# Output projection 1: a third unit of seven block products for the rows from 2048 on

## The chip, the cores and the metric

The kernel runs on one core of a Trainium2 chip. The metric is the device time of one execution in microseconds; the median of three runs of the kernel before is 2237.72 us (2235.79 to 2238.78).

## What is computed

A trunk of two layers on x of 512 x 2048 in float32. The first one, which the change touches, is a gated mixer with a width of 4096:

```python
def spatial_gating_layer(x, norm_g, w_in, v_norm_g, w_s, b_s, w_out):
    h = rms_norm(x, norm_g)
    u, v, z = jnp.split(h @ w_in, 3, axis=-1)      # w_in 2048 x 12288
    u = jax.nn.gelu(u)
    v = rms_norm(jax.nn.gelu(v), v_norm_g)
    ...                                            # v in chunks of 128 positions, 16 groups of 256
    mixed = jnp.einsum('gts,bcsgd->bctgd', w_causal, v) + b_s.T[None, None, :, :, None]
    y = u * mixed * jax.nn.silu(z)                 # 512 x 4096
    return y @ w_out                               # w_out 4096 x 2048: "output projection 1"
```

The second layer is forgetting attention, with an input projection of 2048 x 8208 and its own output projection of 2048 x 2048. Each layer's output is added to x.

## The kernel before

**Precision.** Each large product is made of three matmuls: high part times high part, high times low, low times high (lines 1416 to 1418 in `product`, 1593 to 1595 in `tile`). The high part is a copy in the type fp32r by ScalarE, the low part the difference, by VectorE.

**Units.** Most products run in units of 2048 rows x 1024 columns of weights. A unit does a 2 x 2 block product with seven block products instead of eight. It has 16 steps, one for each pair of row blocks k in each of two phases: 8 steps of four products (24 matmuls of 128 x 512) and 8 steps of three (18 matmuls). Units 0 to 3 (VU = 4) give v, units 4 to 11 give u and z (ZU = 8, so NU = 12), units 12 and 13 (NU, NU+1; `is_out`) the output projection for rows 0 to 2047, columns 0 to 1023 and 1024 to 2047. NS = 14. Units UB and on belong to the second layer.

**One step.** SP loads the weights into one of four raw slots (`load_step`), so it is up to four steps ahead; in the second phase also a sum from t2_rows. VectorE forms a sum in the slot (`sums`), ScalarE makes the high parts (`high`: the first tiles, then the others), VectorE the low parts (`low`: first tiles with line 1877, other tiles with line 1880). TensorE does two products behind `lo1_first` and the rest behind `lo1_ready` (`first_half`, `second_half`). In the instruction order of VectorE, `sums` of the next step stands before both low parts of this step. u_hi and u_lo have two buffers each. `sums_end`, `sum_57`, `sum_11` combine the products in buffers at the unit's end.

**What becomes of y.** y is made in eight parts of 512 columns. Unit VU+1+j gates part j: ScalarE and VectorE make y0, POOL loads v from v_rows (line 734), ScalarE scales it (`v_scale`, line 1047), TensorE mixes it (`mix`, line 1547) and turns it (`turn_y`), ScalarE takes it out of PSUM (`y_leave`) in two halves e. The last half of part j is taken out at the start of the next unit. POOL stores parts 0 to 3 to yf_rows and parts 4 to 7 to yT_rows.

**Forms.** Units 12 and 13 need sums of blocks of y ("forms"). POOL makes them in DRAM: `forms(j, n)` for n = 0 to 4 are five rounds of copies and accumulating DMAs over yf_rows (lines 704 to 714), each of which waits for the one before through the semaphore `made`, 192 a part. They are made for j = 0 to 3, in POOL's loop one part later: behind the store of part j and ahead of the loads of v. Then SP loads them (`load_form(m)`, 8 forms for x1 and 8 for x2) in units NU-1 and NU, at the steps that the tables FORM_LOAD, FORM_HIGH and FORM_LOW give, counted from the start of NU-1: 7, 8, 9, 12, ..., 29 for the load. `load_form(m)` stands behind `load_step` of that step in SP's order; SP runs in order. ScalarE and VectorE make their high and low parts (`form_high`, `form_low`).

**Products into DRAM.** part_rows holds x at first; POOL adds the units' output buffers to it by accumulating DMAs (`store_out`, 512 KB each; semaphore o_stored).

**Plain products.** Rows 2048 to 4095 (KB = 16 row blocks) are done by `tile` for each of the four column blocks f of 512: 64 tiles (B0 = 64), 12 matmuls each. The operands come from yT_rows (`load_y`, `y_high`, `y_low`), the weights through w_raw, w_hi, w_lo. `add_out(f)` adds PSUM and part_rows in acc[f]. Then acc is turned for the second layer (`turn_x`), its squares are summed, and it is stored in x2_rows.

Stretches of the profile: unit NU-1 begins at about 896 us, NU at 978, NU+1 at 1059; the plain tiles run from 1136 to 1316, then UB begins.

Of the kernel before, what the change touches and what calls it, by code (L numbers as in the profile page):

```python
# [23 lines left out]
F32 = mybir.dt.float32  # L24
# [11 lines left out]
def build_trunk(nc, x, a_norm_g, a_w_in, a_v_norm_g, a_w_s, a_b_s, a_w_out,  # L36
# [23 lines left out]
    NS = NU + D // (2 * FB)  # L60
    STEPS = NS * 2 * KP
    KB = KY - 2 * KP
    B0 = NF * KB
# [31 lines left out]
    yf_dram = nc.dram_tensor("yf_rows", [KP, P, 10, HF], F32).ap()  # L95
# [6 lines left out]
    with ExitStack() as ctx:  # L102
# [343 lines left out]
        def form_step(u, ph, k):  # L446
            return step_of(u, ph, k) - step_of(NU - 1, 0, 0)
# [35 lines left out]
        def _(sp):  # L483
# [9 lines left out]
            def weights(u, row):  # L493
                if u < VU:
                    return a_v[row:row + P, u, :, :]
                if is_out(u):
                    c = (u - NU) * 2 * FB
                    return a_out[row:row + P, c:c + 2 * FB].rearrange("r (s c) -> r s c", s=2)
# [39 lines left out]
            def load_form(m):  # L538

                n, c = FORM0 + m, m % KP  # L540
                if m == 0:
                    sp.wait_ge(made, 4 * 192)
                elif m >= 3:
                    sp.wait_ge(x1h_ready if m - 3 < KP else x2h_ready, KP + (m - 3) % KP + 1)
                sp.wait_ge(step_done, step_of(NU - 1, 0, 0) + m + 1)
                if m < KP:
                    sp.dma_start(y1_raw[:, c, :].rearrange("p (s t) -> p s t", s=4), yf_dram[c, :, 0:7:2, :])\
                        .then_inc(x_loaded[n % 3], 16)
                else:
                    sp.dma_start(z2[:, c, :, :], yf_dram[c, :, 7:10, :]).then_inc(x_loaded[n % 3], 16)  # L550

            def load_y(k):

                if k < 2:
                    sp.wait_ge(t2_stored[k], NS * KP * 8)
                    if k == 0:
                        for e in range(2):
                            sp.wait_ge(yA_stored[e], 16 * ZU)
# [5 lines left out]
            def load(i):  # L564
                f, k = i // KB, 2 * KP + i % KB
# [25 lines left out]
            for u in range(1, NS):  # L591
                for ph in range(2):
                    for k in range(KP):
                        load_step(u, ph, k)
                        if form_step(u, ph, k) in FORM_LOAD:
                            load_form(FORM_LOAD.index(form_step(u, ph, k)))
# [12 lines left out]
            for i in range(R, B0):  # L609
                f, k = i // KB, i % KB  # L610
                load(i)
                if f == 0 and k + 3 < KB:
                    load_y(k + 3)
                if f == 0 and 4 <= k < 12:
                    if k == 4:
                        sp.wait_ge(lo1_ready, STEPS)
                        sp.wait_ge(o_stored, 128)
                    t, c = k % NT, (k - 4) // NT
                    sp.dma_start(acc[c][:, t, :], part_dram[c, :, t, :]).then_inc(acc_loaded, 16)
                elif f == 1 and k < 2 * NT:  # L620
                    if k == 0:
                        sp.wait_ge(o_stored, 192)
# [1864 lines left out]
```

## Time and profile before

| | |
|---|---|
| Median of the runs | 2237.72 us |
| The profiled execution | 2240.24 us |
| Its span | 2238.5 us |
| TensorE busy | 2213.6 us, 99% |
| VectorE busy | 1716.0 us, 77% |
| ScalarE busy | 1155.0 us, 52% |
| GpSimd busy | 232.5 us, 10% |
| DMA | 520.68 MB, mean 233 GB/s |

The span is the time from the first to the last instruction of the profile. PE is TensorE, DVE VectorE, ACT ScalarE, POOL GpSimd; SPq, ACTq are queues that issue DMAs. In rows in order of time, "[4.57 <-DMA ...]" is the time that the engine stood idle before the instruction, and what ended it. Matmuls overlap, so the busy time of one is longer than its distance to the next.

### The profile page before, as it was taken

To read this page: it belongs to the slowest core of one execution; us is meant where nothing else is said; L and a number is where in the kernel's file an instruction comes from. 1 tells how busy PE (TensorE), PEld (TensorE's weight loads), DVE (VectorE), ACT (ScalarE), POOL (GpSimd) and SP (SyncE) were. 2 spreads that over 40 slices of the span, in tenths; PEclk is the share of its full clock that TensorE was granted. 3 is DMA by queue.
4 is the path that set the end of the run, shared out by engine and by line. 5 is a ranking of instruction groups with operands and counts; after the bars stand their busy time and mean duration, and the time that the engine had idled before them with its cause. 6 is when DMAs were issued, how large, how long until landed. Compare 5 with 4: busy or idle time off the path is not lost.

```text
span 2238.5 us, 27080 instructions
## 1 busy us (share of the span) xinstructions
PE 2213.6 (99%) x10197; PEld 1832.3 (82%) x10197; DVE 1716.0 (77%) x2085; ACT 1155.0 (52%) x1651; POOL 232.5 (10%) x321
## 2 busy tenths in 40 slices
PE   8999999999999999999999999999999999999999
PEld 6888888888888888888888878888788888888887
DVE  8978878877877887898753388976977878677666
ACT  6756645554554554665442455554564555443432
POOL 0011001001201200000000000110210210221110
PEclk9999999999999999999999999999999999999999
DMA  8788877778988976898985455686787798765333
GB/s 287 235 268 273 255 252 250 247 259 264 283 275 258 288 244 215 279 296 270 261 239 149 129 172 181 211 256 209 213 284 228 210 295 254 260 247 162 124 99 122
DMA packets 253793, 520.68 MB, mean 233 GB/s; under 512 B 21536, under 2 KB 37504, under 8 KB 252640
## 3 DMA queue, kind: packets, MB, share of 16 engines
q1 hardware_dynamic: 198800, 383.31, 55.8%
q0 software_dynamic: 29424, 89.47, 12.5%
q10 hardware_dynamic: 25440, 46.17, 5.4%
q8 instruction: 81, 1.33, 0.2%
q14 instruction: 48, 0.39, 0.1%
HBM read 427.58 MB, written 104.01 MB: 237 GB/s over the span
## 4 chain that ended last, share of the span: by engine, by line
PE 90%; DVE 4%; DMA 3%; ACT 1%; issue 1%; ACTq 0%; SPq 0%; POOL 0%; DVEq 0%
PE ps L1416 23%; PE ps L1418 23%; PE ps L1417 23%; PE ps L1807 2%; PE ps L1805 2%; PE ps L1806 2%; PE ps L1593 2%; PE ps L1594 2%; PE ps L1595 2%; PE ps L1721 2%; DMA raw<-in_b_w_in_dram 1%; PE ps L1667 1%; PE ps L1547 1%; DVE u_lo L1877 1%; DVE raw L1856 1%
## 5 line engine op out<-in xcount | busy, mean ns | idle before, releaser
L905 ACT ACTIVATE u_hi<-raw 128x1024 fp32r<-128x1024 f32 x352 | 372.3, 1058 | 452.8 <-PE ps L1418 355.4
L1416 PE MATMUL ps<-u_hi,x1h 128*128 128x512 f32 x1408 | 552.1, 392 | 8.8 <-DVE u_lo L1877 6.3
L1877 DVE TENSOR_TENSOR u_lo<-raw,u_hi 128x1024 fp32r<-128x1024 f32 x352 | 429.7, 1221 | 160.6 <-ACT u_hi L905 159.7
L1417 PE MATMUL ps<-u_lo,x1h 128*128 128x512 f32 x1408 | 549.5, 390 | 0.0
L1418 PE MATMUL ps<-u_hi,x1l 128*128 128x512 f32 x1408 | 549.3, 390 | 0.0
L1416 PE MATMUL ps<-u_hi,x2h 128*128 128x512 f32 x1056 | 418.0, 396 | 0.8 <-ACT e L987 0.7
L910 ACT ACTIVATE u_hi<-raw 128x512 fp32r<-128x512 f32 (+1 forms) x352 | 297.6, 845 | 230.4 <-PE ps L1418 191.7
L1418 PE MATMUL ps<-u_hi,x2l 128*128 128x512 f32 x1056 | 411.6, 390 | 0.0
L1417 PE MATMUL ps<-u_lo,x2h 128*128 128x512 f32 x1056 | 411.1, 389 | 0.0
L1880 DVE TENSOR_TENSOR u_lo<-raw,u_hi 128x512 fp32r<-128x512 f32 (+1 forms) x352 | 335.0, 952 | 41.7 <-ACT u_hi L910 40.5
L1416 PEld LDWEIGHTS ps<-u_hi,x1h 128*128 128x128 f32 x1408 | 265.2, 188 | 67.8 <-DVE u_lo L1877 9.0
L1418 PEld LDWEIGHTS ps<-u_hi,x1l 128*128 128x128 f32 x1408 | 265.3, 188 | 55.5
L1417 PEld LDWEIGHTS ps<-u_lo,x1h 128*128 128x128 f32 x1408 | 265.4, 188 | 54.2
L1856 DVE TENSOR_TENSOR raw<-raw 128x1024 f32<-128x1024 f32 x176 | 214.3, 1218 | 30.5 <-DMA raw<-in_b_w_in_dram 27.6
L1416 PEld LDWEIGHTS ps<-u_hi,x2h 128*128 128x128 f32 x1056 | 198.3, 188 | 41.8 <-issue 1.6
L1418 PEld LDWEIGHTS ps<-u_hi,x2l 128*128 128x128 f32 x1056 | 198.2, 188 | 41.8
L1417 PEld LDWEIGHTS ps<-u_lo,x2h 128*128 128x128 f32 x1056 | 198.4, 188 | 39.8
L1858 DVE TENSOR_TENSOR raw<-raw 128x512 f32<-128x512 f32 x176 | 121.6, 691 | 12.2 <-DMA raw<-t_rows 12.2
L2120 DVE TENSOR_TENSOR w_lo<-w_raw,w_hi 128x512 fp32r<-128x512 f32 x64 | 44.0, 691 | 98.3 <-ACT w_hi L1140 98.3
L2422 DVE TENSOR_TENSOR accb<-ps,accb 128x1024 f32<-128x1024 f32 x64 | 78.2, 1222 | 47.2 <-PE ps L1807 47.1
L1870 DVE TENSOR_TENSOR t<-raw 128x512 f32<-128x512 f32 x160 | 109.4, 684 | 0.7
L1805 PE MATMUL ps<-w_hi,y_s 128*128 128x512 f32 x256 | 104.2, 407 | 0.0
(238 smaller groups left out, 2469.6 us busy)
## 6 DMA issues: line engine op xcount, KB each, us to landing
raw<-in_a_w_in_dram SPq DMA_DIRECT2D x280, 512.0 KB, 4.7
raw<-in_b_w_in_dram SPq DMA_DIRECT2D x184, 512.0 KB, 4.9
t_rows<-t ACTq DMA_DIRECT2D x176, 256.0 KB, 5.6
raw<-t_rows SPq DMA_DIRECT2D x176, 256.0 KB, 5.0
raw<-in_a_w_out_dram SPq DMA_DIRECT2D x48, 512.0 KB, 5.6
w_raw<-in_a_w_out_dram SPq DMA_DIRECT2D x64, 256.0 KB, 3.4
w_raw<-in_b_w_out_dram SPq DMA_DIRECT2D x64, 256.0 KB, 2.9
vz<-vz_rows POOLq DMA_DIRECT2D x16, 512.0 KB, 5.4
```

What stands on the lines that cost most here:

```text
L905: act.activation(first_tiles(hi), first_tiles(m), ACT.Copy).then_inc(hi1_first, 1)
L910: act.activation(other_tiles(hi, u, ph), other_tiles(m, u, ph), ACT.Copy).then_inc(hi1_ready, 1)
L1416: pe.matmul(dst[:, t, :], a, u_hi[:, s, pos, :], start=first, stop=False, skip_group_check=more)
L1417: pe.matmul(dst[:, t, :], a, u_lo[:, s, pos, :], start=False, stop=False, skip_group_check=more)
L1418: mm = pe.matmul(dst[:, t, :], b, u_hi[:, s, pos, :], start=False, stop=last, skip_group_check=more)
L1805: pe.matmul(dst[:, t, :], a, w2_hi[:, n % R, :], start=(k == 0), stop=False)
L1856: dve.tensor_tensor(m[:, 0:2, :], m[:, 0:2, :], m[:, 1:3, :], ALU.add).then_inc(t_ready, 1)
L1858: dve.tensor_tensor(m[:, 0, :], m[:, 3, :], m[:, 2, :], ALU.subtract if is_out(u) else ALU.add)\
L1870: dve.tensor_tensor(t2[:, q % 2, :], raw_of(g)[:, 0, :], raw_of(g)[:, 2, :], ALU.add)\
L1877: dve.tensor_tensor(first_tiles(lo), first_tiles(m), first_tiles(hi), ALU.subtract)\
L1880: dve.tensor_tensor(other_tiles(lo, u, ph), other_tiles(m, u, ph), other_tiles(hi, u, ph), ALU.subtract).then_inc(lo1_ready, 1)
L2422: dve.tensor_tensor(o, (pP, pX)[th], o, ALU.add).then_inc(half_added, 1)
```

## The change

- NS grows by one: unit 14 (NU+2) does rows 2048 to 4095, columns 0 to 1023 with seven block products. The plain products are left for columns 1024 to 2047 of these rows (F0 = 2; 32 tiles instead of 64).
- All eight parts of y are stored to yf_rows; parts 4 to 7 also to yT_rows. The middle blocks get a negative sign in both; `y_high` and `y_low` turn it back, in two instructions of half the width each.
- `forms` are made for all eight parts: j = 4, 5 and 6 in POOL's loop, j = 7 behind the stores of unit NU's products. The same three tables give the steps for the second set of 16 forms, 32 steps later (units NU+1 and NU+2). Its first load waits for `made` to reach 1536.
- part_rows 0 and 1 are complete in DRAM after unit NU+2's accumulating stores, which wait for those of unit NU; they are loaded into acc 0 and 1 with no addition from PSUM.
- `low` is split in two: in nearly all units (1 to 14 and those behind UB) the low part of the first tiles now stands before the next step's sum, that of the other tiles after it.

The core of the diff:

```diff
-    NS = NU + D // (2 * FB)
+    NS = NU + D // (2 * FB) + 1
...
-    B0 = NF * KB
+    F0 = NF // 2
+    B0 = (NF - F0) * KB
...
-        def form_step(u, ph, k):
-            return step_of(u, ph, k) - step_of(NU - 1, 0, 0)
+        def form_at(table, u, ph, k):
+
+            n = step_of(u, ph, k) - step_of(NU - 1, 0, 0)
+            for m in range(2):
+                if n - m * 4 * KP in table:
+                    return m * 2 * KP + table.index(n - m * 4 * KP)
+
+        def y_stores(j):
+
+            return 16 * (j + max(j - 4, 0))
...
             def load_form(m):
 
-                n, c = FORM0 + m, m % KP
-                if m == 0:
-                    sp.wait_ge(made, 4 * 192)
-                elif m >= 3:
-                    sp.wait_ge(x1h_ready if m - 3 < KP else x2h_ready, KP + (m - 3) % KP + 1)
-                sp.wait_ge(step_done, step_of(NU - 1, 0, 0) + m + 1)
+                n, c, r = FORM0 + m, m % KP, m // (2 * KP)
+                x1_form = m % (2 * KP) < KP
+                if m % (2 * KP) == 0:
+                    sp.wait_ge(made, (r + 1) * 4 * 192)
+                    sp.wait_ge(x2h_ready, (r + 1) * KP)
+                elif m % (2 * KP) >= 3:
+                    sp.wait_ge(x1h_ready if m % (2 * KP) - 3 < KP else x2h_ready, (r + 1) * KP + (m - 3) % KP + 1)
+                sp.wait_ge(step_done, step_of(NU - 1 + 2 * r, 0, 0) + m % (2 * KP) + 1)
...
-                if 1 <= j <= 4:
+                if j > 0:
                     for e in range(2):
-                        pool.wait_ge(yA_stored[e], 16 * j)
+                        pool.wait_ge(yA_stored[e], y_stores(j))
                     for n in range(5):
                         forms(j - 1, n)
...
-                    if j < 4:
-                        pool.dma_start(yf_dram[2 * j + e, :, 2:9:2, :], turned).then_inc(yA_stored[e], 16)
-                    else:
+                    pool.dma_start(yf_dram[2 * j + e, :, 2:9:2, :], turned).then_inc(yA_stored[e], 16)
+                    if j >= 4:
                         c = 4 * j + 2 * e - 2 * KP
                         pool.dma_start(yT_dram[c // 2, :, :, :], turned).then_inc(yA_stored[e], 16)
             for b in (1, 3, 2):
                 store_out(NU, b)
-            for b in (0, 1, 3, 2):
-                store_out(NU + 1, b)
+            for e in range(2):
+                pool.wait_ge(yA_stored[e], y_stores(ZU))
+            for n in range(5):
+                forms(ZU - 1, n)
+            for u in (NU + 1, NU + 2):
+                if u == NU + 2:
+                    pool.wait_ge(o_stored, 192)
+                for b in (0, 1, 3, 2):
+                    store_out(u, b)
...
                 for k in range(KP):
+                    low_first(u, 1, k)
                     if k + 1 < KP:
                         sums(u, 1, k + 1)
                     elif u + 1 < NS:
                         sums(u + 1, 0, 0)
-                    low(u, 1, k)
+                    low_other(u, 1, k)
```

## Rows read from the trace of the kernel before

**Rows 1.** page, part 1: busy time of each engine, share, instructions

```profile
PE 2213.6 (99%) x10197; PEld 1832.3 (82%) x10197; DVE 1716.0 (77%) x2085; ACT 1155.0 (52%) x1651; POOL 232.5 (10%) x321
```

**Rows 2.** waits of TensorE: us in total, times, longest

```profile
PE ps L1416 <- DVE u_lo L1877: 6.3, 5, 2.8
```

**Rows 3.** TensorE in order of time, plain products (start us, duration us)

```profile
1141.15 0.39 PE L1593 MATMUL ps<-w_hi,yhl 128*128 128x512 f32 x1
...
1149.31 0.39 PE L1593 MATMUL ps<-w_hi,yhl 128*128 128x512 f32 x1
```

**Rows 4.** SP's queue in order of time, weights of unit NU+1

```profile
1073.40 0.50 SPq L531 DMA_DIRECT2D raw<-in_a_w_out_dram  x1
1082.34 0.38 SPq L534 DMA_DIRECT2D raw<-in_a_w_out_dram  x1
```

**Rows 5.** TensorE in order of time, unit NU+1, second part of step 7

```profile
1100.41 0.39 PE L1416 MATMUL ps<-u_hi,x1h 128*128 128x512 f32 x1
```

**Rows 6.** POOL in order of time: the last store of y

```profile
1060.69 0.73 POOL L748 DMA_DIRECT2D yT_rows<-y  x1 [7.88 <-ACT y L1057]
```

**Rows 7.** DMA issues, 1060.5 to 1063: KB each, us to landing

```profile
yT_rows<-y POOLq DMA_DIRECT2D x1, 512.0 KB, 6.2
...
part_rows<-cA POOLq DMA_DIRECT2D x1, 512.0 KB, 9.4
...
part_rows<-eU POOLq DMA_DIRECT2D x1, 512.0 KB, 16.2
```

**Rows 8.** POOL in order of time: the chains forms(1) and forms(3)

```profile
577.70 1.08 POOL L704 DMA_DIRECT2D yf_rows<-yf_rows  x2 [4.40 <-issue]
...
609.46 1.19 POOL L734 DMA_DIRECT2D cA<-v_rows  x1
...
734.90 0.77 POOL L745 DMA_DIRECT2D yf_rows<-y  x1 [8.29 <-ACT y L1055]
...
740.15 1.08 POOL L704 DMA_DIRECT2D yf_rows<-yf_rows  x2 [3.94 <-issue]
745.41 1.71 POOL L706 DMA_DIRECT2D yf_rows<-yf_rows  x2 [4.17 <-DMA yf_rows<-yf_rows]
...
773.85 1.70 POOL L714 DMA_DIRECT2D yf_rows<-yf_rows  x2 [9.00 <-DMA yf_rows<-yf_rows]
774.94 1.19 POOL L734 DMA_DIRECT2D cA<-v_rows  x1
```

**Rows 9.** forms: issues of 773 to 775, and landings of tile yf_rows

```profile
yf_rows<-yf_rows POOLq DMA_DIRECT2D x2, 128.0 KB, 5.0
...
DMA to landing us min/median/max: 3.2/5.2/10.3
```

**Rows 10.** ScalarE, then TensorE, at the first mix of j = 4

```profile
782.27 1.71 ACT L1047 ACTIVATE cA<-cA,vrstd 128x256 f32<-128x256 f32 x4 [4.57 <-DMA cA<-v_rows]
...
786.56 0.58 PE L1416 MATMUL ps<-u_hi,x2h 128*128 128x512 f32 x1
```

**Rows 11.** page, part 6: DMA issue, KB each, median us

```profile
raw<-in_a_w_out_dram SPq DMA_DIRECT2D x48, 512.0 KB, 5.6
```

**Rows 12.** TensorE in order of time, unit UB: its longest wait

```profile
1328.89 0.50 PE L1416 MATMUL ps<-u_hi,x1h 128*128 128x512 f32 x1 [2.83 <-DVE u_lo L1877]
...
1330.77 0.63 PE L1417 MATMUL ps<-u_lo,x1h 128*128 128x512 f32 x1
```

**Rows 13.** VectorE, then TensorE, in order of time, late weights

```profile
1500.27 1.23 DVE L1856 TENSOR_TENSOR raw<-raw 128x1024 f32<-128x1024 f32 x1 [4.52 <-DMA raw<-in_b_w_in_dram]
1501.42 1.22 DVE L1877 TENSOR_TENSOR u_lo<-raw,u_hi 128x1024 fp32r<-128x1024 f32 x1
...
1502.69 0.50 PE L1416 MATMUL ps<-u_hi,x1h 128*128 128x512 f32 x1 [0.98 <-DVE u_lo L1877]
```

**Rows 14.** stretches: us, busy PE, PEld, DVE, ACT, POOL, PEclk, DMA, GB/s

```profile
948.00:1029.50 81.50, 81.50 (x370) 67.81 (x369) 75.31 (x79) 52.40 (x65) 3.96 (x6) 1.00 0.91 293
...
1100.00:1136.00 36.00, 36.00 (x159) 29.35 (x157) 25.13 (x32) 19.69 (x28) 0.85 (x1) 1.00 0.61 176
```

More of the change, by code:

```diff
@@ L609, in _ @@
             for i in range(R, B0):
-                f, k = i // KB, i % KB
+                f, k = F0 + i // KB, i % KB
                 load(i)
[L612 to L620, printed above, removed]
+                if f == F0:
+                    if k + 3 < KB:
+                        load_y(k + 3)
+                    if 4 <= k < 4 + NT:
+                        if k == 4:
+                            sp.wait_ge(lo1_ready, STEPS)
+                            sp.wait_ge(o_stored, 192)
+                        sp.dma_start(acc[F0][:, k - 4, :], part_dram[F0, :, k - 4, :]).then_inc(acc3_loaded, 16)
+                    elif 10 <= k < 14:
+                        if k == 10:
+                            sp.wait_ge(o_stored, 256)
+                        for t in range(2):
+                            c, n = (k - 10) // 2, (k - 10) % 2 * 2 + t
+                            sp.dma_start(acc[c][:, n, :], part_dram[c, :, n, :]).then_inc(acc_loaded, 16)
+                elif k < NT:
                     if k == 0:
-                        sp.wait_ge(o_stored, 192)
+                        sp.wait_ge(acc3_loaded, 16 * NT)
                         for e in range(2):
-                            sp.wait_ge(yA_stored[e], 16 * ZU)
-                    t, c = k % NT, 2 + k // NT
-                    sp.dma_start(acc[c][:, t, :], part_dram[c, :, t, :]).then_inc(acc3_loaded, 16)
+                            sp.wait_ge(yA_stored[e], y_stores(ZU))
+                    sp.dma_start(acc[NF - 1][:, k, :], part_dram[NF - 1, :, k, :]).then_inc(acc3_loaded, 16)
                 elif f == NF - 1 and k in (10, 14):
@@ L1074, in y_high @@
                     act.wait_ge(step_done, STEPS)
-                act.activation(y_tile(k)[:, 0, :], t2[:, k % 2, :], ACT.Copy).then_inc(yAh_ready, 1)
+                (plus, minus), (m, n) = halves_of(y_tile(k)[:, 0, :], k), halves_of(t2[:, k % 2, :], k)
+                act.activation(plus, m, ACT.Copy)
+                act.activation(minus, n, ACT.Copy, scale=-1.0).then_inc(yAh_ready, 1)
             high(0, 0, 0)
@@ L2148, in _ @@
             sums_end(NS - 1)
-            for f in range(NF):
+            for f in range(F0, NF):
                 for k in range(KB):
-                    if f * KB + k + LEAD < B0:
-                        split(f * KB + k + LEAD)
-                    if f == 0:
+                    i = (f - F0) * KB + k
+                    if i + LEAD < B0:
+                        split(i + LEAD)
+                    if f == F0:
                         if k + 6 < KB:
@@ L2346, in _ @@
                     elif k > 1:
-                        low(u, 0, k)
+                        low_other(u, 0, k)
                     if 0 < k < KP - 1:
@@ L2362, in _ @@
                 for k in range(KP):
+                    low_first(u, 1, k)
                     if k + 1 < KP:
@@ L2373, in _ @@
                             row_logits(1)
-                    low(u, 1, k)
+                    low_other(u, 1, k)
                     if k == KP - 1 and u + 1 < NUT:
```

150 lines of the change are left out of this document (81 added, 69 removed).

## The prediction

> **What bounds the kernel.** I read the page's engine line first: TensorE is busy for 99% of the span, and no other engine passes 77% [rows 1]. So the time is the number of matmuls times their spacing, plus TensorE's idle time. The spacing is not the 390 ns that a matmul's own row shows, since they overlap: from 1141.15 to 1149.31 there are 36 starts, 0.227 us apart [rows 3]. Then I read TensorE's waits. Behind the start-up, the only sizeable ones are for the low part of a weight tile, 6.3 us in five places [rows 2]. Last I read, for the stretch around the change, the queue of SP, the queue of POOL and the DMA landings, because the change puts a new dependency there.
>
> **Products.** Columns 0 to 1023 of rows 2048 on take 16 row blocks x 2 column blocks x 4 token blocks x 3 = 384 plain matmuls. A unit of seven products takes 8 steps of 24 and 8 steps of 18, 336. Both are 512 columns wide. 48 x 0.227 = 10.9 us less [rows 3]. This lies on the bounding engine, so it counts in full. (The Trainium skill, "TensorE: Matmul & The Clock Gate", gives N / 2.4 GHz + 2.5 ns in its part on the clock gate, 0.216 us at 512 columns; by it the saving would be an estimated 10.4 us. The trace shows 0.227 here, and I go by that.) One boundary between units is added and two between plain blocks go; such a boundary has cost TensorE 0.1 to 0.5 us, so I put +0.5 for it and for VectorE's work in the third unit's second half, where the forms' low parts meet the halved low parts of y. That stage has 25.1 us of VectorE work in 36 before [rows 14]; seven low parts of at most 1.2 us and some small overhead still leave it at the edge, so 0 to 3.
>
> **The sum between the low parts.** Where a weight tile lands late, VectorE waits in the sum of the next step and only then does the first low part that TensorE needs: the sum starts at 1500.27 after 4.52 us of waiting, the low part at 1501.42, TensorE at 1502.69 after 0.98 us idle [rows 13]. With the first low part ahead of the sum this wait goes. The 6.3 us of rows 2 are five such waits, but the longest, 2.8 us [rows 12], is in a step of unit UB whose order isn't changed. I put -2.5, between 0 and -3.5. What is late next is the other low part, which the sum now holds up; it is needed half a step later, so it has room in ordinary steps, but see below.
>
> **y stored twice, and forms in three more units.** For j = 5 to 7 POOL now goes through the five dependent rounds of forms before it may load v. In the units that do so now, the chain from the first form to the issue of v is 31.8 us (577.70 to 609.46) to 34.8 us (740.15 to 774.94) [rows 8]. In the latter, ScalarE waits 4.57 us for v; its scale starts at 782.27, and the step behind the mix starts on TensorE at 786.56 [rows 10]. From the landing of v, the scale (1.71), a high and a low part (at most 1.2 each [rows 13]) take 4.1 us, so the cover left is 0.2 us. Now each half of y is stored twice, 512 KB each, so the first round starts some 2 us later. Hence j = 5 costs about 0.8 us, j = 6, with the first half's form loads beside it, about 1.6. In NU (j = 7) the DMA engines are already 91% busy and VectorE 75.3 us of 81.5 [rows 14]; I put 3. Together +5.4; the bounds are 0 (the shortest chain each time) and 12.
>
> **The chain in front of the third unit.** This term decides. The third unit's first form load is put behind the load of step 7 of unit NU+1 and waits until all eight j are formed. SP is in order: queued behind it are the weights of the second half, which SP issues at 1082.34 now, after 1073.40 for step 7 [rows 4]. The last half of y leaves at 1060.69 [rows 6], so the chain starts only then, one microsecond into NU+1. It goes like this:
> - Two stores instead of one. One landed in 6.2 us; behind it on the same queue stand three accumulating stores of products, which landed after 9.4 us to 16.2 us, the last at about 1078.7, some 4 us apiece [rows 6, 7]. The first form can be issued near 1069.5; if it lands behind these stores, that is near 1082.
> - Four rounds more. In the present chain three of them take 28.4 us (745.41 to 773.85), and the last lands 5.0 us after its issue [rows 8, 9]: with an issue, 34.5 us, ending at 1116.5. The shortest form landed in 3.2 us [rows 9]; with 1.7 us of issuing [rows 8] that is 4.9 a round, ending at 1101.6, and at 1094 if the first form need not stand behind the stores.
> - Since SP is stopped, no weight loads compete after about 1083. I take 1105, nearer to the short end.
> - From there: two issues of 0.4, a landing of 5.6 us [rows 11], the 512-wide sum (estimated at 0.7 from 1.23 for 1024) and the other low part of step 7 (1.2 [rows 13]), which the new order puts behind that sum. TensorE gets on 8 us after the chain's end. It arrives at this low part at 1100.41 [rows 5]. So the idle time is 1105 + 8 - 1100.4 = 12.6 us, with bounds of 1.6 and 24.
> - After the wait of 2.83 us at 1328.89, eight matmuls started 0.43 apart instead of 0.227, at the lower level of the clock (1.2 GHz); the row of 1330.77 with 0.63 us is one [rows 12]. That is 1.6 us; for a longer wait I put 2.
>
> **Sum.** Against the profiled execution (2240.24 us; its span is 2238.5 and 1.7 lie around it): -10.9 - 2.5 + 0.5 + 5.4 + 12.6 + 2.0 = +7.1, 2247.3. The median of the runs is 2.5 us below the profiled execution, so the timed median would be 2244.8 us.
>
> Edits that I cost at nothing: the new sign in y's leaving (done for j < 4 now, with no wait of TensorE), the two halves in y_high and y_low (beside plain tiles of 12 matmuls, 2.7 us each), the parts 0 and 1 loaded whole instead of added in PSUM, and the squares for the norm, moved one block forward. They hide behind the 32 plain tiles left, 87 us. Without that cover, a transition such as the loads of acc would cost its landing, about 5 us, once.
>
> **Rivals.**
> - The chain is fast enough. If it ends by 1092.4, nothing waits. For this, five rounds of the shortest landing alone, 3.2 us [rows 9], behind the landing of y at 1060.69 + 6.2 = 1067 would end at 1083, before TensorE needs anything. Against it speaks that each of the present chains needs over 31 us [rows 8]. The time would be 2237.7 - 10.9 - 2.5 + 1 to 3 for j = 7, 2227. The Trainium skill ("DMA: Bandwidth & Descriptors", on the anatomy of one DMA) has 2.0 us + bytes / 436e3 per DMA, which gives 2.3 us for a form of 128 KB; by that the chain would be hidden. The trace disagrees with a shortest landing of 3.2 and a median of 5.2. Chance 0.14.
> - The chain ends between 1093 and 1100, and the v loads stay nearly covered: 2237.7 - 10.9 - 2.5 + 4 + 1.5 + 3 = 2233. It needs the idle DMA engines to halve the rounds. Chance 0.14, half of it faster by over 0.2%, half within.
> - DMA is what is full. In NU its share is 0.91 [rows 14], and the forms of j = 6 come on top; loads of weights then come late all through NU and NU+1, the scale of v holds up ScalarE's high parts, and the chain ends at 1115 or later. It decides once a weight load takes over the three steps (16 us) by which SP is ahead. 2237.7 - 10.9 + 12 + 22 + 2.5 = 2263. Chance 0.10.
> - The new order doesn't remove the waits of rows 2, because the weights themselves are late: then 2.5 us more than each case. It is within the ranges.
>
> **How the numbers follow.** My forecast, chain ending at 1100 to 1115 with small waits for v, has 0.62 and gives 2237 to 2259; of this 0.50 is slower by over 0.2% and 0.12 within. (0.2%, 4.5 us, is about what a measurement can tell from no change.) With the rivals: faster 0.21, same 0.19, slower 0.60. The range of 8 in 10 reaches from the second rival's lower side to the forecast's upper end: 2230 to 2259.
>
> **What the profile would show.** Right: in SP's queue a gap of over 20 us between step 7's weights of NU+1 and the second half's, ended by a form's landing; TensorE idle once near 1100 for 6 to 24 us behind the low part of L1880's line, with half-clock matmuls after it; 48 matmuls fewer; a short wait of TensorE behind each mix of j = 5 to 7. Wrong: if that gap ends before 1092, or if TensorE has no wait above 3 us between 1060 and 1140, the chain's term fails and the kernel is faster by some 11 us. If the wait at 1502 is still there, the order of the sum did nothing.

## The result and the profile after

| | before | after |
|---|---|---|
| Median of the runs | 2237.89 us | 2262.8 us |
| Ratio, 95% interval | | 1.0103 [1.0089, 1.0116] |
| The profiled execution, its span | 2240.24, 2238.5 us | 2261.33, 2259.5 us |
| Granted clock of TensorE, mean | 0.999 | 0.994 |

By the ratio the change costs 23 us, 1.0% (24.9 us between the two medians, 21.0 between the two spans). The forecast was 2244.8 us with a range to 2259: the direction is right, the size is outside the range. (One of the four runs of the changed kernel, at a granted clock of 0.656, took 3180 us and is left out of the ratio; the median of the other three is 2262.68.)

The page of the changed kernel, part 1; it answers to [rows 1]:

```profile
PE 2208.9 (98%) x10149; PEld 1826.0 (81%) x10149; DVE 1761.0 (78%) x2142; ACT 1183.2 (52%) x1694; POOL 279.0 (12%) x381
```

There are the 48 matmuls fewer that the prediction counted, and the span is 21.0 us longer in spite of them. So TensorE has become idle, or slow. Its waits (us in total, times, longest), against the one entry of 6.3 us in [rows 2]:

```profile
PE ps L1446 <- DVE u_lo L1917: 17.1, 1, 17.1
PE ps L1446 <- DVE u_lo L1910: 8.2, 6, 2.6
...
PE ps L1577 <- ACT cA L1077: 2.9, 2, 1.5
...
PE ps L1696 <- DVE e L1994: 1.6, 1, 1.6
...
PE ps L1446 <- ACT eU L1030: 1.1, 1, 1.1
```

L1910 and L1917 are the low parts of the first and of the other tiles (1877 and 1880 before), L1577 is the mix. One wait of 17.1 us stands out. For the rest I took four marks that both traces have: the start of NU+1, the start of the next unit or tile (336 matmuls later in both), the wait of 2.6 us in UB ([rows 12] before), and the end.

| stretch | before | after | difference | predicted |
|---|---|---|---|---|
| up to the start of NU+1 | 1059.1 | 1069.6 | +10.5 | +5.4 |
| NU+1 | 77.2 | 96.2 | +19.0 | +14.6 (12.6 idle, 2.0 clock) |
| from there to UB's wait: 64 plain tiles, or NU+2 and 32 | 192.6 | 184.8 | -7.8 | -10.4 |
| UB's wait to the end | 909.6 | 909.0 | -0.6 | -2.5 |
| sum | | | +21.0 | +7.1 (as in the sum) |

(The prediction's -2.5 for the order stands in the last line, since the waits of [rows 2] lie at UB's wait and behind it: at 1328.89, 1335.31, 1502.69, 1578.54 and 1821.00.)

**The stretch in front of NU+1.** TensorE in order of time, its waits from 940 to 1045:

```profile
950.00 1.97 PE L1577 MATMUL ps<-cA,ws_t 128*128 128x256 f32 x8 [1.53 <-ACT cA L1077]
953.06 0.50 PE L1446 MATMUL ps<-u_hi,x2h 128*128 128x512 f32 x1 [1.09 <-DVE u_lo L1910]
1000.00 0.74 PE L1446 MATMUL ps<-u_hi,x1h 128*128 128x512 f32 x1 [2.23 <-DVE u_lo L1910]
1038.63 1.97 PE L1577 MATMUL ps<-cA,ws_t 128*128 128x256 f32 x8 [1.39 <-ACT cA L1077]
1041.48 0.50 PE L1446 MATMUL ps<-u_hi,x2h 128*128 128x512 f32 x1 [0.89 <-DVE u_lo L1910]
```

At 950 and 1038 the mix waits for v's scale: the chain of forms in front of the v loads is too long for its cover, as predicted. Here is the chain of forms(6) on POOL, from the two stores of y (first two lines) to the load of v (last line), to be read beside [rows 8]:

```profile
982.83 0.78 POOL L766 DMA_DIRECT2D yf_rows<-y  x1 [7.51 <-ACT y L1084]
983.59 0.75 POOL L769 DMA_DIRECT2D yT_rows<-y  x1
...
994.69 1.09 POOL L726 DMA_DIRECT2D yf_rows<-yf_rows  x2 [9.80 <-issue]
...
1028.96 1.69 POOL L736 DMA_DIRECT2D yf_rows<-yf_rows  x2 [10.03 <-DMA yf_rows<-yf_rows]
1030.04 1.19 POOL L756 DMA_DIRECT2D cA<-v_rows  x1
```

The chain itself, 994.69 to 1030.04, is 35.4 us, close to the 34.8 before. But it starts 11.9 us after the first store (11.1 after the second), where [rows 8] had 5.3 (734.90 to 740.15). That is 6.6 us later; I had allowed 2 us for the second store.

The wait at 1000.00 I had not foreseen. ScalarE, then VectorE, in order of time:

```profile
994.24 0.72 ACT L1062 ACTIVATE y<-e,hrstd_a 128x512 f32<-128x512 f32 x1 [4.44 <-DMA yT_rows<-y]
```

```profile
998.72 1.23 DVE L1910 TENSOR_TENSOR u_lo<-raw,u_hi 128x1024 fp32r<-128x1024 f32 x1 [4.76 <-ACT u_hi L935]
```

L1062 is the tanh of the gate; it writes y's buffer anew, so it too waits for both stores of the part before. It stood 4.44 us for the second one, and the high part that a weight tile needs (L935) stands behind it in ScalarE's order. VectorE then waits for that, and TensorE for VectorE.

**The chain in front of the third unit.** POOL in order of time, to be read beside [rows 6]:

```profile
1071.99 0.75 POOL L769 DMA_DIRECT2D yT_rows<-y  x1
...
1073.77 1.66 POOL L742 DMA_DIRECT2D part_rows<-eU  x1
1080.02 1.12 POOL L726 DMA_DIRECT2D yf_rows<-yf_rows  x2 [4.59 <-issue]
1093.56 1.70 POOL L728 DMA_DIRECT2D yf_rows<-yf_rows  x2 [12.42 <-DMA yf_rows<-yf_rows]
...
1113.89 1.69 POOL L736 DMA_DIRECT2D yf_rows<-yf_rows  x2 [4.75 <-DMA yf_rows<-yf_rows]
```

The first copy (1080.02) took 12.4 us until the next round could go; the others took 3.9 to 4.8. It stood behind three accumulating stores, whose landings are (KB each, us; issued 1071 to 1074, beside [rows 7]):

```profile
yT_rows<-y POOLq DMA_DIRECT2D x1, 512.0 KB, 7.5
part_rows<-cA POOLq DMA_DIRECT2D x1, 512.0 KB, 10.5
part_rows<-e POOLq DMA_DIRECT2D x1, 512.0 KB, 13.9
part_rows<-eU POOLq DMA_DIRECT2D x1, 512.0 KB, 17.6
```

SP's queue, beside [rows 4]: the last weights before the form load at 1084.44, then nothing for 34 us.

```profile
1084.44 0.48 SPq L546 DMA_DIRECT2D raw<-in_a_w_out_dram  x1
1118.46 0.38 SPq L564 DMA_DIRECT2D y_raw<-yf_rows  x1
1118.88 0.51 SPq L549 DMA_DIRECT2D raw<-in_a_w_out_dram  x1
1119.43 0.47 SPq L551 DMA_DIRECT2D raw<-t_rows  x1
```

VectorE waits for what was queued behind the form load, not for the form; then TensorE, beside [rows 5]:

```profile
1125.85 0.69 DVE L1887 TENSOR_TENSOR raw<-raw 128x512 f32<-128x512 f32 x1 [22.90 <-DMA raw<-t_rows]
1126.46 1.22 DVE L1917 TENSOR_TENSOR u_lo<-raw,u_hi 128x1024 fp32r<-128x1024 f32 x1
```

```profile
1127.73 0.79 PE L1446 MATMUL ps<-u_hi,x1h 128*128 128x512 f32 x1 [17.07 <-DVE u_lo L1917]
...
1133.02 0.49 PE L1446 MATMUL ps<-u_hi,x2h 128*128 128x512 f32 x1
```

That is the predicted sequence, link by link. Behind the wait, twelve matmuls take 5.3 us (1127.73 to 1133.02), at the lower level of the clock, instead of 2.7.

The busy times and DMA shares of NU and of NU+1, and the stretch that [rows 14] has too (columns as there):

```profile
981.00:1069.70 88.70, 84.19 (x373) 68.98 (x372) 75.46 (x81) 50.53 (x65) 15.56 (x20) 0.98 0.92 290
1069.70:1165.50 95.80, 78.73 (x337) 64.63 (x336) 62.00 (x65) 40.69 (x44) 15.03 (x18) 0.89 0.90 279
1100.00:1136.00 36.00, 18.93 (x73) 15.12 (x72) 12.07 (x14) 8.17 (x9) 6.94 (x8) 0.72 0.73 204
```

### The profile page after: what moved, and what is told of

It is laid out like the page before. It is cut to its first block, busy times and chain, and to the rows that moved or that the text cites. A ratio compares the mean times of both kernels' runs of the same rounds, so it can differ in the third digit from the quotient of the medians.

```text
span 2259.5 us, 27199 instructions
## 1 busy us (share of the span) xinstructions
PE 2208.9 (98%) x10149; PEld 1826.0 (81%) x10149; DVE 1761.0 (78%) x2142; ACT 1183.2 (52%) x1694; POOL 279.0 (12%) x381
## 4 chain that ended last, share of the span: by engine, by line
PE 85%; DMA 6%; DVE 4%; issue 2%; ACT 2%; POOL 1%; ACTq 0%; SPq 0%; POOLq 0%; DVEq 0%
PE ps L1446 22%; PE ps L1448 22%; PE ps L1447 22%; DMA yf_rows<-yf_rows 4%; PE ps L1836 2%; PE ps L1834 2%; PE ps L1835 2%; PE ps L1750 2%; PE ps L1623 1%; PE ps L1625 1%; PE ps L1624 1%; PE ps L1696 1%; DVE u_lo L1910 1%; PE ps L1577 1%; PE ps L1665 1%
## 5 line engine op out<-in xcount | busy, mean ns | idle before, releaser
L935 ACT ACTIVATE u_hi<-raw 128x1024 fp32r<-128x1024 f32 x368 | 389.4, 1058 | 509.6 <-PE ps L1448 327.3
L1910 DVE TENSOR_TENSOR u_lo<-raw,u_hi 128x1024 fp32r<-128x1024 f32 x368 | 449.3, 1221 | 226.3 <-ACT u_hi L935 226.1
L1446 PE MATMUL ps<-u_hi,x1h 128*128 128x512 f32 x1472 | 578.6, 393 | 25.8 <-DVE u_lo L1917 17.1
L1448 PE MATMUL ps<-u_hi,x1l 128*128 128x512 f32 x1472 | 576.1, 391 | 0.0
L1447 PE MATMUL ps<-u_lo,x1h 128*128 128x512 f32 x1472 | 575.9, 391 | 0.0
L1446 PE MATMUL ps<-u_hi,x2h 128*128 128x512 f32 x1104 | 436.5, 395 | 3.9 <-DVE u_lo L1910 2.9
L1448 PE MATMUL ps<-u_hi,x2l 128*128 128x512 f32 x1104 | 430.2, 390 | 0.0
L1447 PE MATMUL ps<-u_lo,x2h 128*128 128x512 f32 x1104 | 429.8, 389 | 0.0
L1917 DVE TENSOR_TENSOR u_lo<-raw,u_hi 128x512 fp32r<-128x512 f32 (+1 forms) x368 | 350.1, 951 | 21.4 <-ACT u_hi L940 20.7
L1885 DVE TENSOR_TENSOR raw<-raw 128x1024 f32<-128x1024 f32 x184 | 224.1, 1218 | 17.6 <-DMA raw<-in_b_w_in_dram 13.5
L1834 PE MATMUL ps<-w_hi,y_s 128*128 128x512 f32 x256 | 104.2, 407 | 0.0
L1836 PE MATMUL ps<-w_hi,y_s 128*128 128x512 f32 x256 | 100.3, 392 | 0.0
```

The lines of the kernel that those rows point to most:

```text
L935: act.activation(first_tiles(hi), first_tiles(m), ACT.Copy).then_inc(hi1_first, 1)
L1446: pe.matmul(dst[:, t, :], a, u_hi[:, s, pos, :], start=first, stop=False, skip_group_check=more)
L1447: pe.matmul(dst[:, t, :], a, u_lo[:, s, pos, :], start=False, stop=False, skip_group_check=more)
L1448: mm = pe.matmul(dst[:, t, :], b, u_hi[:, s, pos, :], start=False, stop=last, skip_group_check=more)
L1834: pe.matmul(dst[:, t, :], a, w2_hi[:, n % R, :], start=(k == 0), stop=False)
L1836: mm = pe.matmul(dst[:, t, :], b, w2_hi[:, n % R, :], start=False, stop=(k == 1))
```

## The experiments

My theory after the result: two costs, separate from each other, and both from the new dependency on y's forms: the v loads behind them (+10.5) and the wait of the third unit's first form load for all eight parts (+19.0). The rivals: the second stores of y are the cause; DMA is full; the order of the low parts; or the third unit itself saves less than counted. Each line with a ratio compares with the kernel before on the same chip.

**Wait for each form by itself** (e1):

```diff
+                sp.wait_ge(made, (4 * r + c // 2 + 1) * 192)
                 if m % (2 * KP) == 0:
-                    sp.wait_ge(made, (r + 1) * 4 * 192)
                     sp.wait_ge(x2h_ready, (r + 1) * KP)
```

> The changed kernel, but each form load waits only for the part of y that it reads, not for all eight parts. Theory: the in-order queue of SP, held at the first form load until the last round of forms has landed, made the weights of unit NU+1's second half late. Then TensorE's wait of 17.1 us and the 2.4 us of half clock behind it go: 2262.8 - 19.5 = 2243 us, and SP's gap before those weights is under 12 us. Rival: the weights were late because the DMA engines were full with forms and accumulating stores; then a wait of over 10 us stays near the same place and the time is above 2256 us.

Measured: 2244.82 us, ratio 1.0032 [1.0021, 1.0043]; 18.0 us less than the changed kernel. SP's queue now has the second set's first form load at 1085.50. Only the seventh, the first one that reads part 7, comes as the last round lands (1129.31):

```profile
1085.50 0.46 SPq L564 DMA_DIRECT2D y_raw<-yf_rows  x1
...
1129.33 0.36 SPq L564 DMA_DIRECT2D y_raw<-yf_rows  x1
```

The wait of 17 us is gone, and unit NU+1 takes 76.8 us instead of 96.2; from its start to the end TensorE waits 5.0 us for u_lo in all. The chain of forms(7) was no shorter here: its fourth round left at 1113.07, later than 1106.85 in the changed kernel. So it is not the length of the chain that costs, but that everything on SP stood behind it. That shows the term of NU+1.

**v loads ahead of the last round** (e2). The fifth round touches no data of v; moving it behind the two v loads takes its wait out of their path:

```diff
-                    for n in range(5):
+                    for n in range(4):
                         forms(j - 1, n)
...
+                if j > 0:
+                    forms(j - 1, 4)
```

> The changed kernel, but POOL issues the loads of v ahead of the last of the five rounds of forms. Theory: the loads of v queued behind the rounds cost the waits at the first mix of j = 6 and j = 7 (1.5 + 1.1 and 1.4 + 0.9 us on TensorE): all four go, 2262.8 - 4.9 = 2258 us, and the wait of 17 us stays. Rival: v is late because the DMA engines are full in these units: the waits shrink by under 2 us, 2261 us or more.

Measured: 2253.76 us, ratio 1.0063 [1.0048, 1.0078]; 9.0 us less, where the theory had 4.9. No mix waits any more, NU+1 starts 10 us earlier, and 0.74 us is left of the wait near 1000, which the theory had not connected with the v loads; why it shrinks with them isn't shown. The 17 us wait is still there with 16.1. So the first term, too, is shown, and the two are separate.

**Parts 4 to 7 stored once** (e3): only to yf_rows, in which the chain's first round also copies one block row to an eleventh row, so that the plain products can be read from there:

```diff
-            return 16 * (j + max(j - 4, 0))
+            return 16 * j
...
                         pool.dma_start(rows_c[:, 0, :], rows_c[:, 2, :]).then_inc(made, 16)
+                        if j >= 4:
+                            pool.dma_start(rows_c[:, 10, :], rows_c[:, 4, :]).then_inc(ws_loaded, 16)
...
-                    if j >= 4:
-                        c = 4 * j + 2 * e - 2 * KP
-                        pool.dma_start(yT_dram[c // 2, :, :, :], turned).then_inc(yA_stored[e], 16)
```

> The changed kernel, but parts 4 to 7 of y are stored once; the one block row that a later round overwrites is kept by a copy of 128 KB a row block beside round 0, and the plain products read these rows. Theory: the second store delayed whoever waits for y's buffer: ScalarE's gate by 4.4 us in unit NU (2.2 us of TensorE's wait and about 2 us of half clock), and each chain's start by 2 to 4 us (at the two mixes and at the wait of 17 us): together -8 us, 2255 us. Rival: only the chain's start counts, -3 us, 2260 us, with the wait near the start of unit NU still there.

Measured: 2260.5 us, ratio 1.0094 [1.0078, 1.0109], 2.3 us less. The time is the rival's, but the wait near 1000, which the rival kept, is gone. So that wait needs the second store. The store alone doesn't make it, though: with both stores in place it is 2.23 us here, 1.25 in e1, 0.38 in e11, and e7 below has none. Nor is the second store the main cause of the rest, since the mixes still waited 0.68 and 3.18 us and NU+1 15.42. (Two extra copies stand in the chain instead of the store, so this run doesn't price the store by itself.) And a new wait appeared in the plain stage. ScalarE, then TensorE:

```profile
1253.13 0.42 ACT L1106 ACTIVATE yhl<-t 128x256 fp32r<-128x256 f32 x1 [7.45 <-DMA t<-yf_rows]
```

```profile
1271.92 0.47 PE L1626 MATMUL ps<-w_hi,yhl 128*128 128x512 f32 x1 [1.59 <-DVE w_lo L2165]
```

**The order of the low parts alone** (e4), in the kernel before:

```diff
                 for k in range(KP):
+                    low_first(u, 1, k)
                     if k + 1 < KP:
                         sums(u, 1, k + 1)
...
-                    low(u, 1, k)
+                    low_other(u, 1, k)
```

> The kernel before with the new order alone: the low part of the first tiles ahead of the next step's sum. My prediction's term: -2.5 us, 2235.4 us. Rival, from the changed kernel's profile, where the distance to the kernel before shrinks by only 0.6 us over the second layer: -0.6 us, 2237.3 us, because other waits of 1 to 2 us appear in the second layer where the short ones go.

Measured: 2239.61 us, ratio 1.0005 [0.9996, 1.0015]: no effect. TensorE's waits in this kernel, beside [rows 2]:

```profile
PE ps L1416 <- DVE u_lo L1881: 3.3, 2, 2.8
...
PE ps L1667 <- DVE e L1965: 1.6, 1, 1.6
...
PE ps L1416 <- ACT eU L1000: 1.1, 1, 1.1
PE ps L1698 <- DVE nmin L2294: 0.7, 1, 0.7
```

The 3 us that I had counted on did go (6.3 became 3.3), and came back elsewhere: the one for e grew from 0.5 to 1.6, those for eU and nmin are new.

**Both repairs together** (e7).

> The changed kernel with both of the edits tried before: each form load of the second set waits only for the rounds that make its own form, and the v loads go ahead of the last round of forms. Theory: the two costs are separate pieces of TensorE's idle time (one is a wait in unit NU+1, the other the delay with which that unit begins), so the savings add: 2262.8 - 18.0 - 9.0 = 2235.8 us, ratio to the kernel before 0.999 (0.997 to 1.001); no wait of TensorE above 1.5 us between 860 and 1150. Rival: the savings overlap, since TensorE now comes to the forms 9 us earlier while their chain hangs on other transfers too; then a wait of some us is back in NU+1 or NU+2, and the time is 2239 to 2243 us, ratio 1.001 to 1.002.

Measured: 2233.71 us, ratio 0.9979 [0.9969, 0.9989]. This one is faster than the kernel before, by 0.2%, and 29 us faster than the changed kernel; the separate gains of 18.0 and 9.0 make 27.0. NU+1 starts where it does before (last turning of y at 1058.35; before 1058.29). TensorE's waits are back to small ones:

```profile
PE ps L1448 <- DVE u_lo L1912: 4.7, 3, 2.6
...
PE ps L1448 <- DVE cA L2007: 1.7, 2, 1.1
```

The largest between 860 and 1150 is 1.08 us, at 1137.99, as expected; ahead of UB one of 1.69 at 1202.57 follows. Unit NU+1 takes 76.3 us, though the DMA share there is 1.07 (0.90 in the changed kernel): full DMA engines don't hold TensorE up in this unit.

**The same with one store of y** (e5).

> The kernel with the first two edits, and parts 4 to 7 of y stored once instead of twice (a copy of 128 KB per block inside the chain instead, the plain products read from yf_rows). One store fewer took a wait of ScalarE's gate away, 1 us in NU, but brought three waits for w_lo in the plain stage, 3.5 us in all. If these add, the time is 2236 to 2239, 1 to 3 us above the kernel with two stores; if the waits for w_lo came only from part stores that were late with the chain, they are gone and it is 1 us below.

Measured: 2237.94 us, ratio 0.9994 [0.9985, 1.0003]: 4 us worse than with two stores. The waits for w_lo came back with 1.8 us, with the chain no longer late. All of the loss is in the plain tiles, 112.5 us up to UB's wait against 107.4 in e7, and the largest wait there is another one: 2.47 us at 1272.67, where acc is turned (0.93 in e7), with matmuls at the lower clock behind it. So the second store, which looked like waste, is the cheaper way here.

**The chain ahead of the stores of products** (e8), in the changed kernel:

```diff
-            for b in (1, 3, 2):
-                store_out(NU, b)
             for e in range(2):
                 pool.wait_ge(yA_stored[e], y_stores(ZU))
             for n in range(5):
                 forms(ZU - 1, n)
+            for b in (1, 3, 2):
+                store_out(NU, b)
```

> The changed kernel with the three accumulating stores of unit NU's products put behind the last chain of forms instead of in front of it; the first form load still waits for all eight parts. Theory: the first copy of the chain was held up by those stores on the same queue (it took 12.4 us to its landing, 4 to 5 us in other rounds). The chain then ends some 9 us earlier, the wait of 17.1 us shrinks to about 8, and the time is 2252 to 2255 us, ratio 1.007. Rival: the copy was slow because the DMA engines are full, or because of y's own second store; then the wait stays at 14 to 17 us and the time at 2260 to 2263, ratio 1.010. The stores leave some 25 us later, and the first of their buffers is written anew near the end of NU+1's first half; if they are late there, VectorE waits and the gain is less.

Measured: 2266.1 us, ratio 1.0123 [1.0109, 1.0136]: 3.3 us slower than the changed kernel, a miss for the theory and for the rival. POOL, then TensorE, then a landing (issues 1060 to 1125):

```profile
1085.45 1.08 POOL L726 DMA_DIRECT2D yf_rows<-yf_rows  x2 [7.89 <-issue]
1092.81 1.70 POOL L728 DMA_DIRECT2D yf_rows<-yf_rows  x2 [6.27 <-DMA yf_rows<-yf_rows]
...
1113.12 1.69 POOL L736 DMA_DIRECT2D yf_rows<-yf_rows  x2 [4.50 <-DMA yf_rows<-yf_rows]
1114.21 1.52 POOL L742 DMA_DIRECT2D part_rows<-cA  x1
```

```profile
1132.07 0.80 PE L1446 MATMUL ps<-u_hi,x1h 128*128 128x512 f32 x1 [16.62 <-DVE u_lo L1917]
```

```profile
y_raw<-yf_rows SPq DMA_DIRECT2D x2, 512.0 KB, 10.4
```

The first copy waits 6.3 us instead of 12.4, so the stores in front of it did hold it up, by 6.2 us. From first to last round the chain is 27.7 us instead of 33.9. But the stores now leave together with the form load and the weights; the first two form loads landed after 10.4 us, against 5.6 in the changed kernel. It took 14.0 us from SP's issue (1118.07) to TensorE's next matmul, where it was 9.3 (1118.46 to 1127.73). So 4.7 of the 6.2 us were given back, and unit NU+1 is 1.5 us shorter than in the changed kernel (94.7 against 96.2). The rest of the loss stands ahead of the edit: NU+1 starts 4.8 us later, because the mixes lost more (below).

**All three moves** (e9).

> All three: form loads that wait for their own form, v loads ahead of the last round, and the chain ahead of the stores of products. If the waits for forms are gone with the first two already, this is within 1 us of the kernel with those two (2235 to 2237). If the last forms are still late there (waits of 1 to 5 us in NU+1's second half and NU+2), it is 2 to 4 us faster: 2232 to 2234, ratio 0.997 to 0.998.

Measured: 2252.55 us, ratio 1.0061 [1.0049, 1.0073], 19 us worse than e7. Neither expectation holds. TensorE, then ScalarE:

```profile
1122.05 0.76 PE L1448 MATMUL ps<-u_hi,x2h 128*128 128x512 f32 x1 [18.13 <-ACT e L1019]
```

```profile
1120.88 1.02 ACT L1019 ACTIVATE e<-ps 128x1024 f32<-128x1024 f32 x1 [21.73 <-DMA part_rows<-eU]
```

To take NU+1's first products out of PSUM, ScalarE waits until all four stores of NU have landed, since they share one semaphore and eU's is the last. It was ready at 1099.15 (1120.88 - 21.73), and the stores leave only at 1108 to 1109. I had taken the due time from the changed kernel, where this line runs at 1128.96, late only because TensorE had stood still. In e7 the last store of NU was issued at 1063.34, landed 18.3 us later, and L1019 ran at 1098.88. The wait that I had removed was also the cover of the stores.

**The products alone** (e10). No forms for j >= 4 and no second store; the second set of form loads reads the first set's forms, so the third unit works on other data of the same size:

```diff
-                    sp.wait_ge(made, (r + 1) * 4 * 192)
+                    sp.wait_ge(made, 4 * 192)
...
-            return 16 * (j + max(j - 4, 0))
+            return 16 * j
...
-                    for n in range(5):
+                    for n in range(5 if j <= 4 else 0):
                         forms(j - 1, n)
```

> The changed kernel without any of the new forms: y parts 4 to 7 are stored once, to yT_rows, as before; no forms for j = 4 to 7; the form loads of the second set read the forms of the first set (same size and number, wrong data) and wait only for those. What is left of the change is the third unit, the second set of form loads, the new order and the two plain column blocks less. Theory: the products term of 9.6 us, measured in the trace of the changed kernel for the stretch behind the waits, holds by itself, the order is worth nothing, and the second layer gave 0.6: 2237.9 - 10.2 = 2227.7 us, ratio 0.9955. Rival: the second set of form loads and VectorE's extra low parts have a price that the waits for the forms have hidden so far; then 2230 to 2234, ratio 0.997 to 0.998, with waits for u_lo in NU+1 and NU+2.

Measured: 2232.4 us, ratio 0.9971 [0.9959, 0.9983], that is 6.5 us less than before (3.8 to 9.2), where I expected 10.2. The span of its profiled execution is 2229.1, 9.4 below that of before; its runs lie from 2230.0 to 2234.9, and the profiled one (2230.96) is at the fast end. (The 9.6 us in the theory was a misreading of mine: I had set the start of NU+2 in the changed kernel at 1167.5 instead of 1165.8. The stretch behind NU+1 gives 7.8, as in the table above.) In the trace the stretch from y's last turning to UB's wait is 261.5 us instead of 270.6: 9.1 less. What is missing to the 10.9 of the products is mostly in two small waits there, 1.00 us at 1201.04 and 0.52 at 1266.36. The median, not the trace, contradicts the full -10.9, and what makes up the rest of it I can't name from one profile.

**The front alone** (e11): e10 with the second stores and the forms of j = 4 to 6 back in place (again with the first set's forms read).

> As the kernel before in this list, but with the second stores of y and the forms of j = 4 to 6 in front of the v loads (mixes of j = 5 to 7), as in the changed kernel; no forms of j = 7, and the second set's loads wait for nothing new. Theory: this part alone delays the start of NU+1 by the 10.5 us seen in the changed kernel: 2238.2 us, ratio 1.000, waits behind the mixes of j = 6 and 7 and one of some 2 us near 1000. Rival: part of those 10.5 us came with the particular phase of the loads; the waits differ from program to program by several us, and the time is anywhere from 2233 to 2242.

Measured: 2247.07 us, ratio 1.0031 [1.0019, 1.0044], 14.7 us above e10. The theory's 10.5 is too small and the rival's range, too. NU+1 starts 13.2 us later than in e10 (last turning of y at 1071.58 against 1058.40). TensorE at the first mix of j = 5, in e11 and in e8:

```profile
869.69 2.77 PE L1573 MATMUL ps<-cA,ws_t 128*128 128x256 f32 x8 [2.41 <-ACT cA L1073]
```

```profile
870.48 2.90 PE L1577 MATMUL ps<-cA,ws_t 128*128 128x256 f32 x6 [4.19 <-ACT cA L1077]
```

The changed kernel has no wait there, and its mix is 0.4 us late; e1, with the same code up to this point, has a wait of 1.8. So the same instructions lose 0.4, 1.8, 2.4 or 4.2 us at this place, and 10.5, 10.8, 13.3 or 15.3 until NU+1. With v ahead (e2, e5, e7, e9, e12) the last turning comes at 1058.4 to 1059.4 every time. I read this as the missing cover: each variation of a landing reaches TensorE. Each program has one profile, so how much of the spread is between programs and how much between runs of one isn't shown.

**The two repairs with the old order** (e12): as e7, but sum first, then both low parts.

> The changed kernel with form loads that wait for their own form and v loads ahead of the last round of forms (2233.7 us), but with the old order: the next step's sum first, then both low parts. Theory: the order is worth nothing here either, since a wait that it takes from the low part of the first tiles comes back at other places: 2233 to 2235 us, ratio 0.997 to 0.9985. Rival: in the third unit, where the forms land late, the order is needed; then 2 us or more are lost: 2236 or above, with waits for u_lo in NU+1 of over 1 us that are not in the other.

Measured: 2237.36 us, ratio 0.9993 [0.9984, 1.0002]. Against e7's 0.9979 that is 0.14% more, with an uncertainty of about the same size from the two intervals; the spans are 2233.9 and 2231.4. A wait of 2.15 us at 1083.56 and one of 2.33 at 1206.95 stand in it, and NU+1 takes 79.2 us against 76.3 in e7; behind UB's wait it is 0.6 us shorter instead. So the rival is nearer: in this kernel the order is probably worth 2 to 3 us; in the kernel before it is worth nothing.

## Why the prediction was wrong

The direction came out, and for the two large terms so did the mechanism; their sizes didn't, and the order's term failed. The span grew by 21.0 us, not 7.1. The missing 14 us are 5.1 in the term for y and its forms, 4.4 in the wait of NU+1 with its clock, 2.6 in the products and 1.9 in the order: four errors to the same side.

- **Products**, -10.9 + 0.5: in the changed kernel's trace it is -7.8 behind NU+1 and another -0.6 in NU+1 itself, once its wait (17.07) and slow matmuls (2.6) are taken off; in e10's trace -9.1. By the medians of e10 it is less, 6.5 with all that belongs to it. So the boundary, VectorE's low parts and the second set of form loads cost 1.8 to 2.4 us by the traces, within the 0 to 3 but not the 0.5 in the sum.
- **Order**, -2.5: failed. "With the first low part ahead of the sum this wait goes" is right (3.0 us of them go in e4), but the time stayed: by e4 the order is worth nothing in the kernel before, and behind UB's wait the changed kernel gained 0.6 us. The wait of [rows 13] is not in the changed kernel, but new ones of 1.1 (eU) and 1.6 us (e) are. I had asked what is late next only within the step, not in the stages behind it.
- **y stored twice and forms in front of v**, +5.4: mis-sized; it measured +10.5 here and up to 15.3 with the same code. By units it is 0.4, 3.2 and 6.9, against 0.8, 1.6 and 3. The missing parts: in NU the chain starts 6.6 us later instead of 2 (11.9 us from the first store to the first form against 5.3); the gate's wait for y's buffer, 2.23 us on TensorE, which I missed because I asked only who waits for v; the wait behind the mix's own (1.09 and 0.89 us), since the next low part comes late too; and the half clock, 1.7 us behind the wait at 1000.00. I had counted the half clock once, for the long wait. Another 0.4 us goes at each mix that waits, and not to the clock, which stayed at its full level there: a wait is counted from the end of the last matmul, but undisturbed the next one starts 0.35 us before that end (949.45 + 0.38, next start 949.48, in the kernel before). (The waits at 1000 to 1042 are 4.5 us, with these 2.1 it is 6.6 of NU's 6.9.) The signs of the prediction had a wait behind each mix of j = 5 to 7; j = 5 had none.
- **The chain in front of the third unit**, 12.6 us idle: mechanism and place right, size 17.07. Counted from the start of NU+1, the chain ended at 1108.0 on the old scale (1118.46 - 10.49) where I took 1105; from there TensorE took 9.3 us, not 8; and it arrived 0.2 earlier. These make the 4.5. The first copy was forecast to land near 1082 and did at 1083.1 (1093.56 - 10.49). The four rounds behind it took 24.9 us; the choice nearer to the short end of 19.6 to 34.5 was a little too near. Its reason holds: in e1, where SP goes on loading weights, the same four rounds take 34.9 us (1094.38 to 1129.31). The Trainium skill ("DMA: Bandwidth & Descriptors", on the anatomy of one DMA) puts a DMA of 128 KB at an estimated 2.3 us; the shortest landing of such a copy in the changed kernel is 2.9 us, the median of its DMAs on yf_rows 5.4.
- **Half clock**, +2.0: 2.6 for this wait; with the 17.1 that is 19.7, and the rest of the unit is 0.6 us shorter than before. The row that I took the price from, [rows 12], doesn't show a cost, though. TensorE has a second wait behind the slow matmuls, and it ends at the same time with and without slow matmuls: 6.42 us after the first in the kernel before, at a granted clock of 0.73 of the full level (a wait of 0.43), and 6.43 us after it in e2, where the clock stayed at 1.00 (a wait of 2.04):

```profile
1341.61 0.50 PE L1448 MATMUL ps<-u_hi,x1h 128*128 128x512 f32 x1 [2.60 <-DVE u_lo L1912]
...
1348.04 0.50 PE L1448 MATMUL ps<-u_hi,x1h 128*128 128x512 f32 x1 [2.04 <-DVE u_lo L1912]
```

- **The range**: its upper end added neither the bounds of the two large terms nor a chance that both are at their upper side. They are linked: both hang on the landings of the same queue. The rival "DMA is what is full", 2263 at 0.10, gave the right time by luck, for a reason that the runs don't bear out: DMA was at 0.92 in NU, but v came late by 1.5 us or less at the mixes and the weights ahead of the form load not at all, and e7 runs with the same transfers at 2233.7, with a DMA share of 1.07 in NU+1.

As a whole: most of the expected gain exists (e10), and two delays cost 29.5 us. Neither is a price of the third unit's own products: one is a wait for all parts where one would do, the other in the main an order on POOL. With both mended the change is faster than before by 0.2%.

## What to carry to other kernels

A wait on a queue that runs in order costs what stands behind it, not what it protects: give each load its own threshold, and put a transfer whose result is needed late behind one that is needed now. When a buffer gets a second reader, list everyone who waits for it to come free, the engine that writes it next among them. And when a stall is to be removed, read the due times of what it covers from a kernel without the stall: in e9 the stores had looked safe only because the stall was there.

## What the runs showed of the hardware

- A copy of 128 KB between DRAM rows took 12.4 us to the next round behind three accumulating stores of 512 KB on the same queue (13.4 in e7, 12.6 in e2), 6.3 without them in front (e8). The stores themselves landed after 10.5, 13.9 and 17.6 us. The Trainium skill ("DMA: Bandwidth & Descriptors", section "Queues, rings and completion order") says of the queues of SP and ScalarE that each DMA engine takes their descriptors in order. On POOL's queue the copies were held up as well, but not to the end of the stores: one of the two (1080.02) landed at 1089.62, the other at 1093.27, the last store at 1091.37.
- Put beside the loads instead, the same three stores raised the landing of the first two form loads, on another queue, from 5.6 to 10.4 us. Moving them moved most of the cost with them.
- The clock can fall to 1.2 GHz after waits of a few us, but doesn't always. In the 13 profiles TensorE has 29 waits of 2.0 to 4.2 us behind its start-up; the granted clock was down during the matmuls behind 19 of them and stayed at 1.00 behind 10, among these one of 3.18 us (e3, at 1035.41), one of 2.88 (e2, at 1222.01) and the one of 2.60 above. Waits of the same code in UB, 2.60 us each, are on both sides (e1 down, e2 and e8 not). What decides isn't shown.
- Where it fell: after the wait of 2.23 us at 1000.00, eight matmuls started 0.43 to 0.54 us apart instead of 0.227; after 17.07 us it was twelve. After waits of 2.41 (e11) and 4.19 us (e8) at the mix, the two mixes of j = 5 started 11.65 and 12.64 us apart instead of 9.90 (866.48 to 876.38 in the kernel before), 1.8 and 2.7 us more, with no further wait between them. There a wait cost 1.6 to 1.8 times its length. In UB, in the kernel before, it cost nothing beyond its length, since a later wait took the slow matmuls up (6.42 and 6.43 us, see above).
- Programs with the same instructions up to a point differ there by up to 4 us where transfers are on the path, and repeated runs of one program spread by 2 us (e2, e3) to 9 us (e1, 2243.65 to 2252.91). One profile of one program doesn't give the price of such a place. That the programs themselves differ is likely for e8: its four runs (2265.6 to 2268.3) are all above the changed kernel's three (2261.3 to 2262.9), and it starts NU+1 4.8 us later though its edit comes behind that point.
